# Chunk recurrence: the transpose of the block inverse is updated beside the inverse, and both heads are seeded before keys and values are scaled

## The reference

```python
kk = jnp.einsum('bhnid,bhnjd->bhnij', k, k)
a_mat = jnp.where(strict, beta[..., :, None] * kk * decay, 0.0) + jnp.eye(chunk, dtype=jnp.float32)
...
w_v = solve(v * beta[..., None])
w_k = solve(k * (beta * jnp.exp(G))[..., None])
...
def step(S, inp):
    wv, wk, qkn, qd, kd, gt = inp
    u = wv - jnp.einsum('bhck,bhkv->bhcv', wk, S)
    o = jnp.einsum('bhck,bhkv->bhcv', qd, S) + jnp.einsum('bhij,bhjv->bhiv', qkn, u)
    S = S * gt[..., None, None] + jnp.einsum('bhck,bhcv->bhkv', kd, u)
    return S, o
```

## Time and profile before

| | us |
|---|---|
| median of 3 runs | 3991.21 (3987.98 to 3994.84) |
| the profiled execution's own time | 3988.52 |
| its span | 3986.4 |
| TensorE busy in the span | 3005.8 |
| VectorE busy | 2474.6 |
| ScalarE busy | 1535.0 |
| GpSimd busy | 1289.7 |

### The profile page before, as it was taken

One profiled execution on the slowest core, in us unless ns is written; L12 is line 12 of the kernel. 1 busy time (PEld: TensorE's weight loads), 2 busy tenths in 40 slices (PEclk: granted clock), 3 DMA queues, 4 the chain that ended last, 5 costly groups with the idle time before them and its releaser, 6 DMA issues. The chain is left out here.

```text
span 3986.4 us, 45941 instructions
## 1 busy us (share of the span) xinstructions
PE 3005.8 (75%) x14557; PEld 1439.4 (36%) x14557; DVE 2474.6 (62%) x6084; ACT 1535.0 (39%) x4402; POOL 1289.7 (32%) x1172
## 2 busy tenths in 40 slices
PE   7997888777666677768757798776777876666666
PEld 6886775322212122223313575322232222222221
DVE  2665443676676667767773343476677677667675
ACT  2352121444343344446432221344544444334332
POOL 0004330444434333333441110233334344334433
PEclk9998788988778788888878898888888988787778
DMA  2211002999999999999996453799999999999998
GB/s 89 73 51 55 13 13 71 404 420 416 420 414 418 405 397 387 411 366 384 402 421 244 165 204 144 291 375 390 381 375 415 405 404 421 413 420 413 411 421 334
DMA packets 234350, 1261.33 MB, mean 316 GB/s; under 512 B 32008, under 2 KB 71952, under 8 KB 97552
## 3 DMA queue, kind: packets, MB, share of 16 engines
q0 software_dynamic: 153600, 1133.58, 69.8%
q1 hardware_dynamic: 80528, 125.08, 9.1%
HBM read 1244.25 MB, written 14.19 MB: 316 GB/s over the span
## 5 line engine op out<-in xcount | busy, mean ns | idle before, releaser
L1951 PE MATMUL acc<-ring,diag 128*64 128x512 f32 x4096 | 1339.0, 751 | 751.3 <-ACT diag L1650 748.9
L1569 POOL DMA_INDIRECT ring<-in_uv,idx x1024 | 1119.1, 1093 | 1895.3 <-PE acc L1951 1635.2
L1761 DVE SCALAR_TENSOR_TENSOR ring<-ring,rep 128x1024 f32<-128x1024 f32 x1024 | 1230.6, 1221 | 368.9 <-DMA ring<-in_uv,idx 309.3
L1951 PEld LDWEIGHTS acc<-ring,diag 128*64 128x64 f32 x4096 | 250.3, 158 | 1494.2 <-ACT diag L1650 1317.8
L1642 ACT ACTIVATE hg<-hs 128x1 f32<-128x1 f32 x1024 | 203.7, 199 | 1141.1 <-DVE ring L1761 1139.1
L1650 ACT ACTIVATE diag<-const,hgg 128x64 f32<-128x64 f32 x1024 | 356.4, 348 | 33.4
L1646 ACT ACTIVATE hgg<-hg,weigh_by 128x1 f32<-128x1 f32 x1024 | 302.0, 295 | 33.2
L1883 PE MATMUL big<-xnT,w 128*128 128x264 f32 (+1 forms) x960 | 297.1, 435 | 0.0
L1883 PEld LDWEIGHTS big<-xnT,w 128*128 128x128 f32 x960 | 174.8, 203 | 185.0 <-issue 166.4
L298 PE MATMUL acc<-xnT,w 128*128 128x260 f32 x1024 | 230.2, 386 | 0.7 <-ACT inp L419 0.7
L298 PEld LDWEIGHTS acc<-xnT,w 128*128 128x128 f32 x1024 | 196.3, 192 | 38.4 <-issue 7.5
(11 more groups left out here) (571 smaller groups left out, 4057.7 us busy)
## 6 DMA issues: line engine op xcount, KB each, us to landing
w<-in_w_peer SPq DMA_DIRECT2D x64, 512.0 KB
w<-in_w_gdn SPq DMA_DIRECT2D x32, 512.0 KB, 3.6
ring<-in_uv,idx POOLq DMA_INDIRECT x1024, 12.3
wo<-in_w_mla_out SPq DMA_DIRECT2D x8, 1024.0 KB, 11.5
wo<-in_w_uq SPq DMA_DIRECT2D x8, 768.0 KB, 14.2
out_ssm_s<-states SPq DMA_DIRECT2D x4, 1024.0 KB, 5.1
wo<-in_w_gdn_out SPq DMA_DIRECT2D x4, 1024.0 KB, 8.2
sk<-in_keys SPq DMA_DIRECT2D x64, 64.0 KB
```

The source lines that it names most:

```text
L1569: pool.indirect_dma_start(out=ring[:, c % RING, :], out_offset=None, in_=uv, in_offset=bass.IndirectOffsetOnAxis(ap=idx[u % 2][:, c:c + 1] ...
L1761: dve.scalar_tensor_tensor(ring[:, c % RING, 0:D], ring[:, c % RING, 0:D], 1.0, rep[:, 2 * a + c // RING, :], ALU.mult, ALU.mult, accum_ou ...
L1951: last = pe.matmul(acc[i][rows(j), :], diag[:, r, :], ring[:, r, D + HALF * j:D + HALF * j + HALF], start=r == 0, stop=r == RING - 1)
```

## The change

`T`, the inverse itself, is no longer made anew at each level by turning `U`. It is turned once, as a whole, from the seed (`flipped`, `flip_out`). After that each of levels 0 to 4 adds to `T` what it adds to `U`, transposed: four more 128x64 matmuls per head, `some(pC, U, X)`, behind those into `pB`, and one more VectorE addition (`paired_up`), ahead of the one for `U`. The next level's `joined` waits for `paired_up`, and `stepped` waits for `grown`. The turns and the copies of `T` of levels 1 to 5 are gone. Second, VectorE makes the product and the seed of both heads first and then `Kb`, `kd`, `Vb` and `qk` of each.

```diff
@@ scalar
+                    for a in range(2):
+                        after(act, at("flipped", i, a + 1))
+                        act.activation(T[a][:, :, :], pC[a][:, :, :], ACT.Copy).then_inc(s["flip_out"], 1)
                     for j in range(LV):
-                        for a in range(2):
-                            after(act, at("flipped", i, 2 * j + a + 1))
-                            act.activation(half(T[a], j, 0), half(pC[a], j, 0), ACT.Copy).then_inc(s["flip_out"], 1)
@@ tensor
+                    for a in range(2):
+                        after(pe, at("seeded", i, 2 * a + 2))
+                        turn(pC[a], U[a]).then_inc(s["flipped"], 1)
                     for j in range(LV):
                         for a in range(2):
-
-                            after(pe, at("seeded", i, 2 * a + 2) if j == 0 else at("grown", i, 2 * (j - 1) + a + 1))
-                            turn(pC[a], U[a]).then_inc(s["flipped"], 1)
-                        for a in range(2):
-                            after(pe, at("flip_out", i, 2 * j + a + 1), at("lmask", i, 2 * j + a + 1))
+                            after(pe, at("paired_up", i, 2 * (j - 1) + a + 1) if j else at("flip_out", i, a + 1), at("lmask", i, 2 * j + a + 1))
...
-                            some(pB[a], X[j % 2][a], U[a], j, 1).then_inc(s["stepped"], 1)
+                            if j:
+                                after(pe, at("grown", i, 2 * (j - 1) + a + 1))
+                            last = some(pB[a], X[j % 2][a], U[a], j, 1)
+                            if j < LV - 1:
+                                last = some(pC[a], U[a], X[j % 2][a], j, 0)
+                            last.then_inc(s["stepped"], 1)
@@ vector
                         dve.tensor_tensor(nA[a][:, :, :], pC[a][:, :, :], nA[a][:, :, :], ALU.mult).then_inc(s["products"], 1)
-                        dve.tensor_tensor(qk[a][:, :, :], pD[a][:, :, :], dec[a][:, :, :], ALU.mult).then_inc(s["products"], 1)
-                        after(dve, at("products", i, 2 * a + 1))
+                        after(dve, at("products", i, a + 1))
                         dve.tensor_tensor(U[a][:, :, :], nA[a][:, :, :], mask(C_LEVEL), ALU.mult).then_inc(s["seeded"], 1)
                         after(dve, at("seeded", i, 2 * a + 1))
                         dve.tensor_tensor(U[a][:, :, :], U[a][:, :, :], mask(C_ID), ALU.add).then_inc(s["seeded"], 1)
+                    for a in range(2):
+                        h = 2 * i + a
                         after(dve, at("turned", i, a + 1))
...
                         dve.tensor_tensor(Vb[a][:, :, :], pB[a][:, :, :], col(0, h), ALU.mult).then_inc(s["scaled"], 1)
+                        dve.tensor_tensor(qk[a][:, :, :], pD[a][:, :, :], dec[a][:, :, :], ALU.mult).then_inc(s["products"], 1)
                     for j in range(LV):
                         for a in range(2):
                             after(dve, at("stepped", i, 2 * j + a + 1))
+                            if j < LV - 1:
+                                dve.tensor_tensor(half(T[a], j, 0), packed(pC[a]).rearrange("p (b s) -> p b s", s=2 << j), half(T[a], j, 0), ALU.add).then_inc(s["paired_up"], 1)
                             dve.tensor_tensor(half(U[a], j, 1), packed(pB[a]).rearrange("p (b s) -> p b s", s=2 << j), half(U[a], j, 1), ALU.add).then_inc(s["grown"], 1)
```

More of the change, by code:

```diff
@@ L510, in gdn_seq @@
     with Marks(core, "seq", rowed=4, summed=2, diff=4, decay=4, masks=4, made=2, signed=2,
-               crossed=2, turned=2, products=4, scaled=6, seeded=4, flipped=2 * LV, flip_out=2 * LV, lmask=2 * LV, joined=2 * LV,
+               crossed=2, turned=2, products=4, scaled=6, seeded=4, flipped=2, flip_out=2, paired_up=2 * (LV - 1), lmask=2 * LV, joined=2 * LV,
                joined_out=2 * LV, stepped=2 * LV, grown=2 * LV, wk=2, wk_out=2, u_made=2 * NT, u_out=2 * NT, s_made=2 * NT,
@@ L574, in _ @@
                             if j == 0:
-                                after(pool, at("products", i, 2 * a + 1))
+                                after(pool, at("products", i, a + 1))
                             if j >= 2:
```

## The result

The changed kernel takes 4039.98 us (median of 4 runs, 4030.76 to 4042.79), the kernel before, run beside it, 3989.64 us. The ratio is 1.012, with a 95% interval of 1.0101 to 1.0139: 40 to 55 us slower. The profiled execution of the changed kernel took 4030.76 us (span 4028.7), the lowest of the four.

The account below looks back on a forecast made before the run. TensorE's own issues were taken to bound the levels. Pair 0's 6.0 us and 3 x 10.7 for the others gave 38 us, 4026.5 from the profiled 3988.5 or 4029 on the median; with 1 us added, 4030, range 4016 to 4046.

Parts of the forecast that it names:

- TensorE's issues are the limit of the levels: Recurrence levels: TensorE's own issues set the pace, not the waits of 4.0 us; a level takes 5.3 us.
- The price: Levels of the recurrence: some 12 us of the 38 us loss are TensorE's added issues, 0.111 us each at full clock.
- The seeds: Before level 0: head 1's seed comes 6th, not 11th, so `stepped` starts 1.1 us sooner a pair (0.3 to 1.9).
- The clock: Levels and behind `read`: half clock lasts until 3 us into `change` or `wk`; the loss beyond some 12 of 38 us.
- The first rival: Levels and behind `read`: any dense run brings the clock back as before; 11.6 us slower, 4003 us; chance 0.07.
- The second rival: Behind `change` of level 2: the clock also falls among 128x64 issues; 35 us on top, 4064 us; chance 0.06.
- The third: Seed waits: the clock does not fall, levels 0 and 1 run at full price; about -5 us, 3986 us; chance 0.03.
- its 1 us: After `wk`: 1 us added because the scan may start at half clock.
- The 13.6 us: From `read` to `wk`: 64 issues at half clock, 0.21 us each, part of 16.8 us to the end of `wk`.
- the sum: Whole stage: 6.0 us for pair 0 and 10.7 for each of three others, 38 us more in all.

Follow-up runs that it names:

- the filled kernels: Kernel before with `read` and `change` moved earlier and unread transposes in TensorE's seed waits, 3968.48 us; the same schedule with `T` kept, 3983.89 us.
- kept alone: Changed kernel with VectorE back in the old order of seeds and scaling: 4041.17 us, ratio 1.0118.
- control: Changed kernel with 8 unread 128x64 matmuls (16 issues) added behind `joined` of level 0 and behind `read`: 4063.66 us, ratio 1.0164.
- `change` early: Changed kernel with `change` of levels 1 and 2 moved to levels 0 and 1: 4018.55 us, ratio 1.007.
- `read` early: `read` of the pair before moved into TensorE's seed wait: with `T` kept and old seed order 4011.99 us, in the kernel before 3970.73 us.
- the run with turns: Changed kernel with 16 unread transposes of a constant added behind `joined` of level 0 and behind `read`: 4018.65 us, ratio 1.006.
- the seeds alone: Kernel before with only VectorE's new order of seeds and scaling, levels still turning `U`: 3992.58 us, ratio 0.9997.
- both early: Kernel before with `read` in the seed wait and `change` at levels 0 and 1: 3968.01 us, ratio 0.9939.
- filled with `T` kept: `T` kept level by level, old seed order, `read` and `change` moved earlier, unread transposes in TensorE's seed waits: 3983.89 us, ratio 0.9979.

## Why the prediction was right

Forecast 4030 (4016 to 4046), measured 4039.98; forecast about 40 us more than before, measured 40 to 55. The stage was forecast at about 387 us and is 392.6.

**TensorE's issues are the limit of the levels.** Right. With `T` kept one `joined` follows another by 5.36 us at full clock (forecast 5.3; two such levels and `joined` of a third fill 12.50 us of the profile after without a gap: 112 issues at 0.1116). The groups of the changed kernel, 308 to 690 us, have the 320 issues that were added, and no wait for `U` or `T` in the levels:

```profile
L626 PE MATMUL pB<-U,X 128*128 128x64 f32 x384 | 67.9, 338 | 0.0
...
L626 PE MATMUL pC<-X,U 128*128 128x64 f32 x320 | 54.2, 325 | 0.0
```

The price, forecast at 12 us, was 11.5 (some 4 either way) by the stage less the clock's share, and 15.4 by the medians of the filled kernels.

**The seeds.** The mechanism was right: from the first product to `stepped` of level 0 it was 13.47 us in pair 1 before (394.94 to 408.41), and the same in pair 0 (317.14 to 330.61). In pair 0 of the changed kernel it was 12.44, which is 1.03 us less against 1.1 forecast:

```profile
317.46 0.68 DVE L761 TENSOR_TENSOR nA<-pC,nA 128x512 f32<-128x512 f32 x1
...
325.88 1.94 PE L626 MATMUL pA<-T,gU 128*128 128x64 f32 x8 [0.78 <-ACT T L592]
...
328.27 1.94 PE L626 MATMUL pA<-T,gU 128*128 128x64 f32 x8 [0.45 <-DVE Vb L771]
...
329.90 1.83 PEld L626 LDWEIGHTS pB<-U,X 128*128 128x128 f32 x8
```

What I had not named is the 0.78 us for ScalarE's copy of the whole of `T`. It costs nothing, since head 1's `joined` waits for `Vb` anyway. Alone this part is worth too little to be seen in the time.

**The clock.** Right, and shown from both sides: the same number of issues gives 45 us between transposes and 128x64 matmuls (4018.65 and 4063.66), and moving `change` alone gives 21. In the five profiles that keep `T` and have no added transposes (changed kernel, kept alone, control, `change` early, `read` early) all 32 rises in the levels came 2.0 to 5.2 us after the start of a `change` or a `wk`, none ahead of one. The first rival, that any dense run brings the clock back, falls with the control. The Trainium skill's sentence that transposes do not count ("TensorE: Matmul & The Clock Gate", Part 4, PE-mode transpose) falls with the run with turns, where they brought the clock back in all seven places. The second rival did not happen: 12.5 us of dense 128x64 issues without a turn ran at 1.00. The third did not either: level 0 ran at 0.50 throughout.

**Sizes.** The delay from the start of `change` to the rise was forecast at 3 us. It was 3.1 to 3.4 in pair 0, 4.6 to 4.9 in pair 1, and much the same again in pairs 2 and 3. From the start of `wk` 3 was forecast too. In pair 1 it was between 2.0 and 2.5, but in pair 2 between 4.1 and 4.5 (561.00 to 565.10 at 0.50), so that the scan there began at half clock, for which the prediction had guessed its 1 us. `read` was taken to stay at 5.41 us; in pair 1 it took 4.2, since more of it ran at full clock. These offset in part. The 13.6 us in the sum are written as 64 x 0.21, which is 13.4; an issue at half clock is nearer 0.213 (3.41 us for 16), and 13.59 was measured. For pair 1 the way from `stepped` of level 0 to `read` grew by 7.6 us (24.97 before, now 413.64 to 446.21); without the seeds' 1.1 us I had forecast 6.2. The stage as a whole grew by 43.3 us against 38 in the sum.

What is left open: the medians differ by 50 us and the stages of the two profiled executions by 43. The profiled execution of the changed kernel was the fastest of its four, and what the others lost, in the stage or outside, no profile shows.

Two more things are open. The prediction's rule that the clock is back some 3 us after the turns or `change` begin is not a fixed one. In seven places of four other profiles it took 7.5 to 15.8 us: three in the seeds alone, two with `read` early, one with both early, one filled with `T` kept. The kernel before had none such in its one profile, so the 31.8 us of clock are those of two executions; that the clock decides rests on the runs with turns, with the control and with `change` early. And why transposes and 128x128 matmuls bring the clock back and 128x64 ones do not, no run separates: only these forms were tried.

## What to carry to other kernels

Before a dependent chain is shortened, look at whether its engine is idle at all: here the chain's wait was 4 us in the stage, and the recomputation that looked wasteful was half the issues of what replaced it. On TensorE count issues and not flops, and look at which work stands where the granted clock comes back; taking it away can cost more than the issues do. Work that brings the clock down is best put where TensorE waits anyway: that alone gave 0.5% here (0.9954, 0.9937 to 0.9971). Work that brings it up is best put at the start of a dense stretch: that gave 0.5% in the changed kernel, and no gain that can be told from none in the kernel before, where turns followed anyway.

## What the runs showed of the hardware that was not expected

A stretch in which TensorE is busy 100% of the time can stay at half clock for 13.7 us (the control, 128x64 in fp32) and also hold full clock for 12.5 us, with the same instructions; which it is depends on what went before. Transposes and 128x128 matmuls brought the full clock back 1.9 to 5.4 us after they began in most places, but not reliably: in seven places it took 7.5 to 15.8. An issue of 128x64 and one of 128x128 take the same time: at full clock 16 of `change` go by in 1.79 us (348.84 to 350.63 in the changed kernel), and 16 of `joined` in 1.78. Executions scatter outside of the part that was changed: the span less the stage was 3636 us in the changed kernel's profile, 3629 in that of the kernel before with `read` early and 3648 in that of the control, so a difference under some 20 us between single profiles can lie outside of the change, and is read from the stage. The stage scatters too, by where the clock comes back, as the seeds alone show.
